# Router logits computed tile by tile inside the output projection of a mixture-of-experts block

## The reference, cut to what matters

```
aff = softmax(h @ w_router)                  # h: 1024 tokens x 1024, w_router: 1024 x 16
gate, idx = top_k(aff.T, 128)                # per expert: values and token numbers
xe = h[idx]                                  # rows gathered, per expert
hid = silu(xe @ w_gate) * (xe @ w_up)
ye = (hid @ w_down) * gate
x = x + gt2 * scatter_add(ye at idx)
```

## Time and profile before

| | |
|---|---|
| runs, median (lowest to highest) | 4555.55 us (4554.89 to 4560.6) |
| profiled execution, its own time | 4555.46 us |
| its span (first to last instruction) | 4553.7 us |
| TensorE busy | 4085.1 us (90%) |
| VectorE busy | 2751.7 us (60%) |
| ScalarE busy | 1061.5 us (23%) |
| GpSimd busy | 624.7 us (14%) |
| granted TensorE clock, mean | 0.95 of full speed |
| output projection with norm, tail | 2301 to 2328 us (layer 0), 3758 to 3784 us (layer 1) |
| routing stage | from 2328.44 us (layer 0), from 3784.03 us (layer 1) |

### The profile page before, as it was taken

One profiled execution on the slowest core, in us unless ns is written; L12 is line 12 of the kernel. 1 busy time (PEld: TensorE's weight loads), 2 busy tenths in 40 slices (PEclk: granted clock), 3 DMA queues, 4 the chain that ended last, 5 costly groups with the idle time before them and its releaser, 6 DMA issues. The chain is left out here.

```text
span 4553.7 us, 42006 instructions
## 1 busy us (share of the span) xinstructions
PE 4085.1 (90%) x14834; PEld 1979.5 (43%) x14834; DVE 2751.7 (60%) x4336; ACT 1061.5 (23%) x2020; POOL 624.7 (14%) x485
## 2 busy tenths in 40 slices
PE   8999998997899899886849999988999994999996
PEld 3444444693444454445523333334444541333332
DVE  3555554544758433355767777855656466777775
ACT  3335452344010311172221111103210102111111
POOL 1011010200000000093102222210000000222221
PEclk9999999998999999898979999998999996999998
DMA  5121225547546212007238999962012105899995
GB/s 116 45 74 61 69 66 178 150 113 259 148 120 222 65 57 85 5 1 205 69 121 333 343 329 331 331 227 76 26 51 72 51 28 194 326 331 332 348 335 209
DMA packets 495132, 739.92 MB, mean 162 GB/s; under 512 B 131094, under 2 KB 237430, under 8 KB 494968
## 3 DMA queue, kind: packets, MB, share of 16 engines
q1 hardware_dynamic: 470024, 687.46, 44.0%
q0 software_dynamic: 11744, 43.00, 3.4%
q10 hardware_dynamic: 13200, 7.34, 0.5%
HBM read 660.65 MB, written 77.06 MB: 162 GB/s over the span
## 5 line engine op out<-in xcount | busy, mean ns | idle before, releaser
L507 PE MATMUL ps<-hT,pr_w 128*128 128x512 f32 x1344 | 588.7, 595 | 5.1 <-issue 3.8
L507 PEld LDWEIGHTS ps<-hT,pr_w 128*128 128x128 f32 x1344 | 254.3, 191 | 319.8 <-issue 316.9
L3523 PE MATMUL ps<-hA,abp_w 128*128 128x512 f32 (+1 forms) x624 | 252.3, 565 | 0.6 <-DVE bv L3704 0.6
L2742 PE MATMUL ps<-moe_wd,moe_hT 128*128 128x512 f32 x512 | 222.4, 592 | 0.0
L2742 PE MATMUL ps<-X,moe_hT 128*128 128x512 f32 x512 | 222.4, 592 | 0.0
L3523 PEld LDWEIGHTS ps<-hA,abp_w 128*128 128x128 f32 x624 | 118.2, 190 | 130.6 <-issue 127.8
L2847 DVE TENSOR_TENSOR ffn_w12g<-ffn_w12g,ffn_w11g 128x1024 f32<-128x1024 f32 x64 | 78.2, 1222 | 154.0 <-DMA ffn_w11u<-in_moe_w_up 154.0
L2742 PEld LDWEIGHTS ps<-moe_wd,moe_hT 128*128 128x128 f32 x512 | 96.0, 190 | 114.8 <-issue 114.8
L2742 PEld LDWEIGHTS ps<-X,moe_hT 128*128 128x128 f32 x512 | 96.0, 190 | 114.8 <-issue 114.8
L2723 PE MATMUL ps<-ffn_w22g,moe_xg 128*64 128x512 f32 x256 | 124.8, 623 | 18.7 <-POOL moe_xg L2686 17.5
L2354 DVE TENSOR_TENSOR X<-X,ps 128x512 f32<-128x512 f32 x192 | 118.2, 681 | 33.7 <-PE ps L2303 32.5
(11 more groups left out here) (783 smaller groups left out, 8597.0 us busy)
## 6 DMA issues: line engine op xcount, KB each, us to landing
moe_wd<-in_moe_w_down SPq DMA_DIRECT2D x32, 2048.0 KB, 17.4
X<-in_moe_w_down SPq DMA_DIRECT2D x32, 2048.0 KB, 18.5
ffn_w12g<-in_moe_w_gate SPq DMA_DIRECT2D x32, 1024.0 KB, 8.5
ffn_w12u<-in_moe_w_up SPq DMA_DIRECT2D x32, 1024.0 KB, 11.9
ffn_w21g<-in_moe_w_gate SPq DMA_DIRECT2D x32, 1024.0 KB, 12.6
ffn_w21u<-in_moe_w_up SPq DMA_DIRECT2D x32, 1024.0 KB, 14.0
ffn_w11g<-in_moe_w_gate SPq DMA_DIRECT2D x60, 512.0 KB, 10.7
ffn_w11u<-in_moe_w_up SPq DMA_DIRECT2D x60, 512.0 KB, 12.3
```

What stands on the lines that cost most here:

```text
L507: ins = eng.matmul(C.ps[r % NRING][:, :], w[:, (n // 2) % NW, k, (n % 2) * P:(n % 2 + 1) * P], HT[:, k, half * BANK:(half + 1) * BANK], st ...
L2742: ins = eng.matmul(C.ps[6 + half][:, :], hT[:, QK * h + k, :], down(q, h)[:, k, half * BANK:(half + 1) * BANK], start=(h == 1 and k == 0), ...
L3523: ins = eng.matmul(C.ps[4 * (n % 2) + bank][:, 0:wd], w[:, buf[kind], k, i * P:(i + 1) * P], HA[:, k, col:col + wd], start=(k == 0), stop= ...
```

## The change

The logits are computed in the projection stage. The router weights are loaded there, unpadded. After `turn(t)` for t = 2 to 7, TensorE computes the logits of tile t - 2, and at the end those of tiles 6 and 7: eight matmuls each, with the 128x128 piece of `XT` as weights and the 16 columns of the router moving, so that tokens are on partitions at once. They wait for both evacuations of their tile and go to bank 0, at a column that `logit_column` gives, which is the place that the softmax reads. In the routing stage the weights' load, its cleared tile, the matmuls, the copy and the four transposes are gone, and VectorE starts with the row maximum; the barrier between the stages orders it behind the logits. Lines after the change are shifted: products are L2319, `turn` L2265, logits L2275.

```diff
-def stage_seven(nc, C, A, name, LT, rows, K, H, first, gained=False, room=None, extra=None, norm=None, after=None):
+def stage_seven(nc, C, A, name, LT, rows, K, H, first, gained=False, room=None, extra=None, norm=None, after=None, router=None):
...
+        if router is not None:
+            E = router.shape[1]
+            wr, s_wr, s_lg = st.sb("wr", [P, KD, E]), st.sem("router"), st.sem("logits")
...
+            if router is not None:
+                with nc.allow_non_contiguous_dma(reason="short rows"):
+                    eng.dma_start(wr[:, :, :], router.rearrange("(k p) e -> p k e", p=P)).then_inc(s_wr, 16)
             if norm and rows_out is not None:
                 for t in range(NT):
                     eng.wait_ge(s_xn, t + 1)
...
+            def logits(t):
+                if t == 0:
+                    eng.wait_ge(s_wr, 16)
+                eng.wait_ge(s_evv, t + 1)
+                eng.wait_ge(s_eva, t + 1)
+                at = logit_column(t)
+                for k in range(KD):
+                    ins = eng.matmul(C.ps[0][:, at:at + E], XT[:, k, t * P:(t + 1) * P], wr[:, k, :], start=(k == 0), stop=(k == KD - 1))
+                ins.then_inc(s_lg, 1)
...
                         if norm:
                             turn(t)
+                        if router is not None and t >= 2:
+                            logits(t - 2)
             if norm:
                 for t in range(TH, NT):
                     turn(t)
+                    if router is not None:
+                        logits(t - 2)
+            if router is not None:
+                logits(NT - 2)
+                logits(NT - 1)
 
...
+EQ, HP, NJ = 32, 64, NT // 2
+def logit_column(t):
+    h, j = divmod(t, NJ)
+    return HP * j + EQ * h
...
+def stage_route(nc, C, name, E, idx, gate, ahead):
...
-        wr = st.sb("wr", [P, KD, EQ])
-        lgT = st.sb("lgT", [HP, BANK])
...
-        s_w, s_z, s_mm, s_lg, s_lt, s_d, s_e, s_v, s_aff, s_t, s_top, s_t2, s_ls, s_rv = (st.sem(x) for x in (
-            "w", "zero", "mm", "logits", "lturned", "dif", "exp", "dve", "aff", "turned", "top", "turned2", "lists", "reversed"))
+        s_z, s_d, s_e, s_v, s_aff, s_t, s_top, s_t2, s_ls, s_rv = (st.sem(x) for x in (
+            "zero", "dif", "exp", "dve", "aff", "turned", "top", "turned2", "lists", "reversed"))
...
-            eng.memset(wr[:, :, :], 0.0).then_inc(s_z, 1)
             eng.memset(aff[:, :, :, :], 0.0).then_inc(s_z, 1)
             eng.memset(back[:, :], 0.0).then_inc(s_z, 1)
-            eng.wait_ge(s_z, 3)
+            eng.wait_ge(s_z, 2)
...
         @block.sync
         def _(eng):
+            ahead(eng)
+
+        @block.tensor
+        def _(eng):
             eng.wait_ge(s_z, 1)
-            with nc.allow_non_contiguous_dma(reason="short rows"):
-                eng.dma_start(wr[:, :, 0:E], w_router.rearrange("(k p) e -> p k e", p=P)).then_inc(s_w, 16)
-            ahead(eng)
-
-        @block.tensor
-        def _(eng):
-            eng.wait_ge(s_w, 16)
-            for k in range(KD):
-                for half in range(2):
-                    ins = eng.matmul(C.ps[0][EQ * half:EQ * (half + 1), :], wr[:, k, :], HT[:, k, half * BANK:(half + 1) * BANK],
-                                     start=(k == 0), stop=(k == KD - 1), tile_position=(0, EQ * half))
-            ins.then_inc(s_mm, 1)
-            eng.wait_ge(s_lg, 1)
-            for j in range(NJ):
-                ins = eng.transpose(C.ps[1][:, j * HP:(j + 1) * HP], lgT[:, j * P:(j + 1) * P], C.ident[0:HP, 0:HP])
-            ins.then_inc(s_lt, 1)
-            eng.wait_ge(s_z, 2)
             eng.wait_ge(s_aff, 1)
             for j in range(NJ):
                 ins = eng.transpose(C.ps[2][0:HP, j * P:(j + 1) * P], aff[:, j, :, :].rearrange("p h e -> p (h e)"), C.ident[:, :])
...
-            eng.wait_ge(s_z, 4)
+            eng.wait_ge(s_z, 3)
             eng.wait_ge(s_ls, 1)
...
-            eng.wait_ge(s_mm, 1)
-            eng.tensor_copy(lgT[:, :], C.ps[0][0:HP, :]).then_inc(s_lg, 1)
-            eng.wait_ge(s_lt, 1)
-            lg = C.ps[1][:, 0:NJ * HP].rearrange("p (j h e) -> p j h e", j=NJ, h=2)[:, :, :, 0:E]
+            lg = C.ps[0][:, 0:NJ * HP].rearrange("p (j h e) -> p j h e", j=NJ, h=2)[:, :, :, 0:E]
             af = aff[:, :, :, 0:E]
             step(eng.tensor_reduce(mx[:, :, :], lg, AX.X, ALU.max))
-            eng.wait_ge(s_z, 2)
+            eng.wait_ge(s_z, 1)
             eng.tensor_tensor(af, lg, bc(mx), ALU.subtract).then_inc(s_d, 1)
...
-                    norm=(MB, gains[:, 0, 1, 0, :], mod[:, 0, 3 * KD:4 * KD, 0], S.d["xrows"]))
+                    norm=(MB, gains[:, 0, 1, 0, :], mod[:, 0, 3 * KD:4 * KD, 0], S.d["xrows"]), router=A["moe_w_router_2"][0])
...
+                                after=small[1] if part == 0 else None, router=A["moe_w_router_2"][1] if part == PARTS - 1 else None)
...
+        stage_route(nc, C, f"route{l}", E, idx, gate, ahead)
```

More of the change, by code:

```diff
@@ L2448, in norm_gains @@
             step(eng.tensor_tensor(gains[:, l, j, r, :], one[:, j, r, :], ng[:, j, :], ALU.mult))
-def stage_route(nc, C, name, HT, w_router, idx, gate, ahead):
-    E, CAP = w_router.shape[1], 2 * SEQ // w_router.shape[1]
+EQ, HP, NJ = 32, 64, NT // 2
[3 more added lines that the diff above has]
+def stage_route(nc, C, name, E, idx, gate, ahead):
+    CAP = 2 * SEQ // E
     RND = CAP // 8
-    EQ, HP, NJ = 32, 64, NT // 2
     with Stage(nc, name) as st:
-        wr = st.sb("wr", [P, KD, EQ])
-        lgT = st.sb("lgT", [HP, BANK])
         aff = st.sb("aff", [P, NJ, 2, EQ])
@@ L2486, in _ @@
         def _(eng):
-            eng.wait_ge(s_z, 1)
-            with nc.allow_non_contiguous_dma(reason="short rows"):
-                eng.dma_start(wr[:, :, 0:E], w_router.rearrange("(k p) e -> p k e", p=P)).then_inc(s_w, 16)
             ahead(eng)
@@ L4372, in mixer_gmlp @@
                                 norm=(UT, gains[:, 1, 1, 0, :], mod[:, 1, 3 * KD:4 * KD, 0], S.d["xrows"]) if part == PARTS - 1 else None,
-                                after=small[1] if part == 0 else None)
+                                after=small[1] if part == 0 else None, router=A["moe_w_router_2"][1] if part == PARTS - 1 else None)
 def ffn(nc, C, A, S, X, HT, mod, gains, l):
@@ L4389, in ahead @@
                     eng.dma_start(wq[b][m][:, :, :], quarter(W[m], b)[0].rearrange("(k p) c -> p k c", p=P)).then_inc(s_wq[b], 16)
-        stage_route(nc, C, f"route{l}", HT, A["moe_w_router_2"][l], idx, gate, ahead)
+        stage_route(nc, C, f"route{l}", E, idx, gate, ahead)
         stage_moe(nc, C, f"moe{l}", X, HT, S.d["xrows"], S.d["xacc"], idx, gate, gain, shift, *W, S.d["mod"][l, 5 * D:6 * D], wq, s_wq)
```

## The result

| | before | changed |
|---|---|---|
| runs, median (lowest to highest) | 4556.58 us (4551.6 to 4560.6), 20 runs | 4568.72 us (4554.53 to 4575.23), 20 runs |
| ratio of the times | | 1.0023, 95% interval 1.0017 to 1.0029 |
| profiled execution, its own time and span | 4555.46, 4553.7 us | 4572.3, 4570.6 us |
| granted TensorE clock, mean | 0.950 | 0.944 |

The change costs 12.1 us by the medians, 10.5 by the ratio of the two sets of runs (8 to 13 by its interval). The forecast was 4545.2 with a range of 4540 to 4551, and slower by over 0.2% had a chance of 0.06.

A forecast was written before the change was run, and what follows sets the result against it. The prediction took VectorE's routing-stage wait for the router matmuls to bound the kernel. It summed -24.44 - 0.44 + 14.56 = -10.32 us, giving 4545.2 us with a range of 4540 to 4551.

The forecast's parts named there:

- What bounds, and what is removed: Routing stage: VectorE waits 12.3 us for router matmuls; removing the serial chain before the exponential saves 24.44 us over two layers.
- T0: Start of ScalarE's table load, its first routing-stage instruction; forecast 17.37 us after tile 3's transposes start, before 11.80.
- drain: Routing stage: a skill's rule adds about 1.38 us per table load, 2.8 us in all; the forecast left it out.
- Price of a tile: Projection: eight logits matmul calls, 16 records on TensorE, cost 1.71 us per tile, with 1.96 as the other end.
- rival 1: Logits groups' price follows the moving columns: 0.2 us a tile, mostly hidden in gaps, time 4531.9; chance 0.04.
- rival 2: Logits groups cost the price of 144 columns: 1.96 us a tile, 4.0 more, time 4549.2; chance 0.08.
- The 4532.5 beside rival 1: Time if a skill's rule of about 60 cycles per matmul held, 16 records taking an estimated 0.4 us.
- Placement: Projection's tail: logits not hidden behind the first group, TensorE without gap; stage's end moves 7.28 us a layer, 14.56 in two.
- The affinities' wait: Routing stage: VectorE's wait for transposed affinities, 0.78 us in layer 0, 1.22 in layer 1, becomes 0.78 in both: -0.44.
- Rival 3: Expert stage waits for its preloaded weights, issued later in each layer, not for its rows: +13.0, 4568.5; chance 0.02.
- rival 4: Projection's tail at the low clock, narrow groups taking double: +21.5 us in one layer, time 4566.7; chance 0.04.

The follow-up runs named there:

- 128 columns, both forms: Changed kernel with 128 moving columns per logits matmul: router columns eight times (4546.17 us), or 16 router columns and 112 zeros (4545.77 us).
- the second 64-column kernel: Changed kernel with 64 moving columns per logits matmul, the softmax reading the right columns: 4546.27 us, ratio 0.9972 to the kernel before.
- its second trace: The changed kernel run again with no edit: 4565.15 us.
- end128: Changed kernel with all eight logits groups behind the last transposes and 128 moving columns: 4558.65 us, ratio 0.9997 to the kernel before.
- run 16: Not a run label: "run" is a verb, for 16 records in the changed kernel with tokens moving and router as weights: 4539.7 us, ratio 0.9965.

## Why the prediction was wrong

- **What bounds, and what is removed: right.** The exponential starts 1.30 us after T0 (2352.57 to 2353.87), no drain stands between load and activation, and the kernel without logits matmuls gained 23.1 us.
- **Price of a tile: right at the high clock.** A group took 1.70 us (forecast 1.71), so rival 1 (0.2) and rival 2 (1.96) both fell. It hardly follows the moving columns: 16, 32, 64 and 128 of them cost 1.70, 1.71, 1.73 and 1.79. (The 4532.5 beside rival 1 is a slip: 0.4 a tile in that sum gives 4533.1. Nothing hangs on it.)
- **Placement: right at the high clock.** TensorE ran without a gap, and the wait changed sides: VectorE now stands 3.65 us for TensorE. In the kernels whose clock held, tile 3's transposes to T0 took 17.89 (128 columns, both forms) and 17.65 (64) where 17.37 was forecast. They came out at 4546 in all, inside the range that was given.
- **Sizes beside it.** The affinities' wait was 1.22 in both layers and not 0.78, +0.88 on the sum. The text took the shorter wait because TensorE would come out of unbroken work. That doesn't decide it: the second 64-column kernel, whose tail ran at 1.00, waited 1.22 in both layers too, the 128-column ones 0.78. What sets it stays open. Rival 3 did not happen: in layer 0, T0 to the first transposes of the gathered rows is as long as before less what was removed (below).
- **The step that failed** is the dismissal of rival 4: "Against: the tail before ran at 0.97 with TensorE busy 4.37 us of 9.20, and now it has no gap." The text took "no gap" for "high clock". The runs show TensorE busy 22.00 of 22.00 us at 0.50 in both layers of the change, 22.00 and 21.98 in its second trace, and at 1.00 in the same place once the same calls move 64 or 128 columns. The row that warned was in the text: 16 one-column records at the low clock took 3.57 us. It was used to price the rival, and not to ask whether such matmuls can run at the high clock for long. Nothing in the earlier trace rows shows more than one group of them at a time.
- The Trainium skill, "TensorE: Matmul & The Clock Gate", section "HAM oscillation — how this bites in real kernels", puts a falling clock down to TensorE standing idle for data. Here it fell with no idle time, so the measurement decides: absence of gaps isn't enough.
- Rival 4's time, 4566.7, was near to what was measured (4568.72), but by luck, as it took another route: it had one layer low from tile 0's group on (+21.5). In fact both were low, each from the third group on (+10.93 and +11.12).

The first transposes of the gathered rows (`moe_xg`), from the view of that tile; the columns are the number of records, shortest, median and longest in ns, and the first and last start. Of the changed kernel:

```profile
L2726 PE MATMUL ps<-ident,moe_xg x256: 272/273/477, 2402.2 to 4455.4; 128*128 128x128 f32 x128
```

and of the kernel before:

```profile
L2715 PE MATMUL ps<-ident,moe_xg x256: 272/273/476, 2389.5 to 4439.1; 128*128 128x128 f32 x128
```

From T0 it was 2389.5 - 2328.44 = 61.1 us and is 2402.2 - 2352.57 = 49.6: 11.4 less, which is the 11.78 removed less the 0.44 of the wait. So the gather's part didn't move.

Two things stay open. The runs show that the clock goes with the number of moving columns, whatever they hold, but not by what measure it falls, and with no logits it can fall in tails of transposes as well. And one of the change's 20 runs took 4554.53 us with a mean clock of 0.948, and the others 4559.79 to 4575.23. It has no trace. Whether the clock held in one of its layers isn't known.

## What to carry to other kernels

When work on TensorE moves onto the path, price it at both clocks, and don't take a busy TensorE for one at 2.4 GHz: look in the windows for a stretch of the same kind of matmul that is as long as yours, and treat the clock as unknown if there is none. If the weight loads set the pace, more moving columns are nearly free (here 0.09 us on 1.70 for eight times as many), so try the padded form, and better the one with the operands swapped and tiles side by side, before giving a placement up. Read the granted clock of the stretch first when a sum of durations misses by a large part of itself.

## What the hardware showed that was not expected

- TensorE busy 22.00 of 22.00 us at a granted clock of 0.50, and 24.50 of 24.50 at 0.57: matmuls with 16 moving columns neither held nor brought back the high clock, though each was loading 128 columns of weights without a pause (weight loads 21.91 of 22.00 us).
- 112 columns of zeros served as well as real ones (4545.77 and 4546.17 us).
- The clock fell as well in tails of transposes with gaps of about 1 us (1.94 and 1.97 us a set in three kernels), and in the one case with 128-column matmuls behind it, layer 1 of `end128`, it was back at 1.00 within the 16.12 us of their run.
- Two float32 column tiles side by side, each with weights of 32 columns, run 16 records with 128 moving columns in 1.00 us, faster than 16 records with 16 columns over the whole array (1.70).
